# Token projections of two mixers, joined in pairs of 512 moving weight columns

## The reference

```
# first block, each of its two layers
h = rmsnorm(x, mix_pre_g)
proj = h @ w_in                  # 3860 columns, split among four heads groups:
#   gated delta net, differential attention (with rotary q, k),
#   state-space scan, mLSTM
# second block, each of its two layers
proj = modulate(x) @ w_in_2      # 3072 columns:
rq, rk, rv, rg, dq, dk, dv, sq, sk, sv = split(proj)
y = concat(retention(rotate(rq), rotate(rk), rv, rg),
           dilated_attention(rotate(dq), rotate(dk), dv),
           stick_breaking(sq, sk, sv)) @ w_out_2
```

## Time and profile before

| | |
|---|---|
| runs | 2170.27, 2171.44, 2171.54 us; median 2171.44 |
| span of the profiled execution | 2169.3 us; the page gives no whole time for it, the median lies 2.1 us above the span |
| PE busy | 2125.2 us (98%), 12850 matmuls |
| DVE busy | 1653.5 us (76%) |
| ACT busy | 1182.4 us (55%) |
| POOL busy | 73.5 us (3%) |
| HBM read | 444.42 MB, 205 GB/s over the span |

### The profile page before, as it was taken

One profiled execution on the slowest core, in us unless ns is written; L12 is line 12 of the kernel. 1 busy time (PEld: TensorE's weight loads), 2 busy tenths in 40 slices (PEclk: granted clock), 3 DMA queues, 4 the chain that ended last, 5 costly groups with the idle time before them and its releaser, 6 DMA issues.

```text
span 2169.3 us, 34586 instructions
## 1 busy us (share of the span) xinstructions
PE 2125.2 (98%) x12850; PEld 1864.8 (86%) x12850; DVE 1653.5 (76%) x2161; ACT 1182.4 (55%) x1589; POOL 73.5 (3%) x70
## 2 busy tenths in 40 slices
PE   8999999999999999999999999999999999999997
PEld 7888999888888889988888888988888888898886
DVE  6877897787778788977877877867787557876657
ACT  5545545654655574465556546546546445656544
POOL 0000200000000003000000000100000000000000
PEclk9999999999999999999999999999999999999999
DMA  8775322577487642238765775437764555443553
GB/s 313 292 281 204 128 79 98 214 282 279 169 325 267 260 156 98 79 112 315 267 255 215 285 280 205 137 105 281 277 252 171 194 200 213 156 136 137 183 194 145
DMA packets 59413, 446.65 MB, mean 206 GB/s; under 512 B 6977, under 2 KB 7361, under 8 KB 8897
## 3 DMA queue, kind: packets, MB, share of 16 engines
q1 hardware_dynamic: 59328, 445.50, 55.2%
HBM read 444.42 MB, written 1.05 MB: 205 GB/s over the span
## 4 chain that ended last, share of the span: by engine, by line
PE 88%; DVE 7%; ACT 3%; DMA 1%; issue 1%; POOL 0%; SPq 0%; DVEq 0%; ACTq 0%
PE ps L249 28%; PE ps L358 15%; PE ps L254 15%; PE ps L364 8%; PE ps L265 3%; PE ps L307 2%; PE ps L313 2%; PE ps L308 2%; PE ps L339 2%; PE ps L230 1%; PE ps L236 1%; PE ps L231 1%; DVE w_lo L206 1%; DMA raw<-in_g 1%; DVE tok L777 1%; PE ps L1196 1%
## 5 line engine op out<-in xcount | busy, mean ns | idle before, releaser
L206 DVE TENSOR_TENSOR w_lo<-raw,w_hi 128x1024 fp32r<-128x1024 f32 x670 | 813.4, 1235 | 274.6 <-ACT w_hi L199 273.8
L199 ACT ACTIVATE w_hi<-raw 128x1024 fp32r<-128x1024 f32 x670 | 693.7, 1052 | 411.2 <-PE ps L364 133.7
L249 PE MATMUL ps<-hT,w_hi 128*128 128x512 f32 x2688 | 671.3, 392 | 0.5 <-ACT w_hi L199 0.5
L249 PEld LDWEIGHTS ps<-hT,w_hi 128*128 128x128 f32 x2688 | 487.9, 189 | 91.4 <-ACT w_hi L199 1.1
L254 PEld LDWEIGHTS ps<-hT,w_lo 128*128 128x128 f32 x2688 | 366.7, 190 | 26.2
L254 PE MATMUL ps<-hT,w_lo 128*128 128x256 f32 x2688 | 374.8, 282 | 0.0
L358 PE MATMUL ps<-w_hi,act_hi 128*128 128x512 f32 x672 | 208.9, 392 | 0.0
L358 PE MATMUL ps<-w_hi,act_lo 128*128 128x512 f32 x672 | 207.6, 390 | 0.0
L364 PE MATMUL ps<-w_lo,act_hi 128*128 128x512 f32 x672 | 179.6, 389 | 0.0
L2081 DVE SCALAR_TENSOR_TENSOR arena<-arena,cond 128x1024 f32<-128x1024 f32 x144 | 168.5, 1221 | 2.7 <-DMA arena<-in_w_ada 2.7
L358 PEld LDWEIGHTS ps<-w_hi,act_lo 128*128 128x128 f32 x672 | 126.2, 188 | 27.5
(11 more groups left out here) (370 smaller groups left out, 2447.5 us busy)
## 6 DMA issues: line engine op xcount, KB each, us to landing
raw<-in_u SPq DMA_DIRECT2D x88, 1024.0 KB, 4.9
raw<-in_d SPq DMA_DIRECT2D x88, 1024.0 KB, 6.9
raw<-in_g SPq DMA_DIRECT2D x87, 1024.0 KB, 4.8
arena<-in_w_ada SPq DMA_DIRECT2D x48, 1536.0 KB, 7.5
raw<-in_w_in SPq DMA_DIRECT2D x54, 1024.0 KB, 4.9
raw<-in_w_out SPq DMA_DIRECT2D x16, 1024.0 KB, 4.9
rows<-in_rows SPq DMA_DIRECT2D x12, 1024.0 KB, 9.0
arena<-in_con SPq DMA_DIRECT2D x1, 1344.0 KB, 10.8
```

The source lines that it names most:

```text
L199: nc.scalar.activation(w_hi[:, buf, 0:width], raw[:, slot, half * UNIT:half * UNIT + width], ACT.Copy).then_inc(unit_hi, 1)
L206: nc.vector.tensor_tensor(w_lo[:, buf, 0:width], raw[:, slot, half * UNIT:half * UNIT + width], w_hi[:, buf, 0:width].bitcast(F32), ALU.su ...
L249: nc.tensor.matmul(o, h_[:, k, c], hT[:, :, 4 * half + k, :], start=(half == k == 0), stop=False)
```

## The change

In mixer 1 the token tiles 4 and 5 become a pair, in mixer 2 the pairs (2, 3), (4, 5), (8, 9) and (10, 11). The host joins the columns of two weight tiles and cuts the result by rows into four quarters, each of two 128-row chunks by 512 columns, of the same size as a unit; the DMAs and conversions stay as they are. `pair_unit` multiplies a quarter: for token tile 0 four hi matmuls of 512 columns and two lo, then the same for tile 1, 12 in all. Each token tile has a bank of its own. Tile 1's bank is the one that tile n - 1 used, so in the first quarter there is a wait for its copy (`freed`) ahead of token tile 1. At the end of token tile 0 in the last quarter `pair_first` is raised; `evict(n)` waits for it and copies 512 columns of token tile 0, `evict(n + 1)` waits for the end of the unit and copies token tile 1. In ScalarE's stream `evict(n)` of a pair moves behind the conversions of the last quarters and of the first unit or units after them.

```diff
+PAIRS1 = (4,)
+PAIRS2 = (2, 4, 8, 10)
...
+    def pair_unit(pe, B, j, banks, quarter, freed=None):
+        buf = home(B, j)
+        h_, l_ = (w[:, buf, :].rearrange("p (k n) -> p k n", k=2) for w in (w_hi, w_lo))
+        unit_ready(pe, unit_hi, B, j)
+        for tile in range(TILES):
+            o, c = ps[:, banks[tile], :], slice(tile * P, (tile + 1) * P)
+            if tile and freed:
+                freed()
+            for k in range(2):
+                nc.tensor.matmul(o, hT_hi[:, 2 * quarter + k, c], h_[:, k, :], start=(quarter == k == 0), stop=False)
+                nc.tensor.matmul(o, hT_lo[:, 2 * quarter + k, c], h_[:, k, :], start=False, stop=False)
+            if tile == 0:
+                unit_ready(pe, unit_lo, B, j)
+            for k in range(2):
+                last = nc.tensor.matmul(o, hT_hi[:, 2 * quarter + k, c], l_[:, k, :], start=False,
+                                        stop=(quarter == 3 and k == 1))
+            if tile == 0 and quarter == 3:
+                last.then_inc(pair_first, 1)
+        last.then_inc(unit_done, 1)
...
+                elif n in PAIRS1:
+                    pair_unit(pe, B, j, (6 + n % 2, 7 - n % 2), half, None if half else lambda: evicted(n - 1))
+                elif n - 1 in PAIRS1:
+                    pair_unit(pe, B, j, (7 - n % 2, 6 + n % 2), 2 + half)
...
+            elif n in PAIRS1:
+                a.wait_ge(pair_first, l * len(PAIRS1) + (PAIRS1.index(n) + 1))
...
-        evict(4)
         after(T1, "sums")
         nc.scalar.activation(gc, ps[:, 5, 0:24].rearrange("p (a b) -> p a b", a=2), ACT.Copy).then_inc(A1.done("gc"), 1)
         after(V1, "rs")
         nc.scalar.activation(rn, rn, ACT.Sqrt).then_inc(A1.done("root"), 1)
         hi(6)
+        evict(4)
         after(V1, "dec_g")
...
-        evict(2)
         hi(4, (0,))
         after(A2, "e_b")
         nc.scalar.activation(b3, b3, ACT.Ln, bias=one[:, 0:1]).then_inc(A2.done("l_b"), 1)
         hi(4, (1,))
+        evict(2)
         evict(3)
         hi(5)
+        hi(6)
         evict(4)
-        hi(6)
         evict(5)
...
+        hi(10)
         evict(8)
-        hi(10)
         evict(9)
...
+        hi(12)
         evict(10)
-        hi(12)
         evict(11)
```

More of the change, by code:

```diff
@@ L157, in build @@
     proj_evac = sem("proj_evac")
+    pair_first = sem("pair_first")
     pre_t = steps("pre_t", "trans0a trans0b trans1a trans1b")
@@ L1459, in mixer1_act @@
                          8: u[:, 6:8, PAD:], 10: u[:, 8:10, PAD:], 11: u[:, 10:12, PAD:]}
-        token_homes = {4: rope_in[:, :, 0:SEQ], 5: rope_in[:, :, SEQ:512], 12: v_d, 13: z_s, 14: o_m, 15: gate_g}
+        token_homes = {12: v_d, 13: z_s, 14: o_m, 15: gate_g}
         def evict(n):
@@ L1468, in evict @@
             bank = 6 + n % 2
-            if n == SMALL_AT:
+            if n in (4, 5):
+                last = nc.scalar.activation(rope_in[:, n - 4, :], ps[:, bank, :], ACT.Copy)
+            elif n == SMALL_AT:
                 last = nc.scalar.activation(small, ps[:, bank, 0:2 * SMALL].rearrange("p (a b) -> p a b", a=2), ACT.Copy)
@@ L2153, in project @@
                         entry_feature(pe, B, g, 4)
+                elif n in PAIRS2:
+                    pair_unit(pe, B, j, (4 + n % 2, 5 - n % 2), half_, None if half_ else lambda: evicted(n - 1))
+                elif n - 1 in PAIRS2:
+                    pair_unit(pe, B, j, (5 - n % 2, 4 + n % 2), 2 + half_)
                 else:
@@ L2300, in evict @@
         def evict(n):
-            a.wait_ge(unit_done, B + (ENDS2[n] + CREDIT))
-            two = ps[:, 4 + n % 2, :].rearrange("p (a b) -> p a b", a=2)
+            if n in PAIRS2:
+                a.wait_ge(pair_first, DEPTH * len(PAIRS1) + (l * len(PAIRS2) + (PAIRS2.index(n) + 1)))
+            else:
+                a.wait_ge(unit_done, B + (ENDS2[n] + CREDIT))
+            bank, tile = ps[:, 4 + n % 2, :], n % 2
+            two = bank.rearrange("p (a b) -> p a b", a=2)
             func, scale = ACT.Copy, 1.0
             if n < 2:
-                to, scale = sqk[:, 2 * n:2 * n + 2, :], 1.0 if n else 64.0 ** -0.5
+                to, from_, scale = sqk[:, 2 * n:2 * n + 2, :], two, 1.0 if n else 64.0 ** -0.5
             elif n < 6:
-                at = (n - 2 + 2) % 4 * SEQ
-                to = rot_in[:, :, at:at + SEQ]
+                at = n // 2 % 2 * 512
+                to, from_ = rot_in[:, tile, at:at + 512], bank
             elif n < 8:
-                to = v_b if n == 6 else v_2
+                to, from_ = v_b if n == 6 else v_2, two
             elif n < 10:
-                to = v_r[:, :, (n - 8) * SEQ:(n - 7) * SEQ]
+                to, from_ = v_r[:, tile, :], bank
             else:
-                to, func = g_r[:, :, (n - 10) * SEQ:(n - 9) * SEQ], ACT.Silu
-            nc.scalar.activation(to, two, func, scale=scale).then_inc(proj_evac, 1)
+                to, from_, func = g_r[:, tile, :], bank, ACT.Silu
+            nc.scalar.activation(to, from_, func, scale=scale).then_inc(proj_evac, 1)
         def hi(n, halves=(0, 1)):
@@ L2802, in column_tiles, with joined @@
                                 .reshape(L_, n // width, P, -1))
+def joined(tiles, first):
+    L_, n, p, _ = tiles.shape
+    for i in first:
+        both = np.concatenate([tiles[:, j].reshape(L_, p, KT, FB) for j in (i, i + 1)], 3)
+        tiles[:, i], tiles[:, i + 1] = (both[:, :, k:k + KT // 2].reshape(L_, p, -1) for k in (0, KT // 2))
+    return tiles
 def row_tiles(w):
@@ L2819, in layout @@
     big = [0, 256, 512, 1032, 1288, 2828, 3084, 2056, 3340, 2312, 2568, 1544, 1800, 3596, 768]
-    a["w_in"] = column_tiles(np.concatenate([w[:, :, c:c + 256] for c in big], 2))
+    a["w_in"] = joined(column_tiles(np.concatenate([w[:, :, c:c + 256] for c in big], 2)), [n - 1 for n in PAIRS1])
     ws = np.concatenate([w[:, :, 1024:1028], w[:, :, 3852:3856], w[:, :, 1028:1032], w[:, :, 2824:2828],
@@ L2825, in layout @@
     w = i["w_in_2"]
-    a["w_in_2"] = column_tiles(np.concatenate([w[:, :, c:c + 256] for c in
-                                               (2304, 2560, 1536, 1792, 0, 256, 2816, 2048, 512, 768, 1024, 1280)], 2))
+    a["w_in_2"] = joined(column_tiles(np.concatenate([w[:, :, c:c + 256] for c in
+                                                      (2304, 2560, 1536, 1792, 0, 256, 2816, 2048, 512, 768, 1024, 1280)],
+                                                     2)), PAIRS2)
     a["w_out_2"] = row_tiles(i["w_out_2"])
```

## The result

The changed kernel takes 2179.52 us in the median (2178.45 to 2180.84, 5 runs) against 2171.44 before: a ratio of 1.0039 with a 95% interval of 1.0028 to 1.005. It is slower, by more than the 0.2% that can be told, and above my range (2171.5 to 2177.8). The profiled execution took 2180.84 us, with a span of 2179.1: 9.8 us more than before, where the sum said 3.7. It is the slowest of the five; the median rose by 8.1. Three single executions further down took two to four times as long (4276 us with mixer 1 undone, 4729 with copy 10 early, 8110 with the pairs 8 and 10 alone); nothing here explains them, and medians and ranges are those of the other executions.

What follows compares the result with a forecast made beforehand. TensorE, 88% of the chain, was taken to bound the kernel. Mixer 1's +3.1 and mixer 2's +0.6 gave +3.7 us on a 2169.3 span, 2173.0; with 2.1 to the median, 2175.1 us (8 in 10: 2171.5 to 2177.8).

Steps and rivals of the forecast that it cites:

- Saved on TensorE: 12 matmuls of 512 columns for 24 of 256 save 0.15 us a changed unit, 6.0 us over 40 units.
- a saving of 2.5 ns a matmul: The skill's issue-gap rule on TensorE: 480 dropped matmuls save only 1.2 us, total about 2179 us; not followed.
- New wait 1: Mixer 1, middle of unit 4a: TensorE waits for tile 3's copy, stalls 2.16 us; +1.56 us a pass.
- rival 1: Mixer 1: GpSimd's later mask and rotations hold VectorE, 1.0 to 2.2 us a pass, 2177.1 to 2179.5 us; chance 0.20.
- New wait 2: Mixer 2, before tile 4: TensorE waits for tile 2's copy, stalls 2.49 us; net +1.10 us a pass.
- the pairs (8, 9) and (10, 11): Mixer 2: nine more units save 1.35 us a pass; entry waits covered; 0.57 us stall before the transposes after tile 11.
- the GpSimd wait: Mixer 2, after unit 5a: TensorE's old 0.34 us wait for GpSimd's mask goes, the mask being ready first.
- a drain behind each table load: ScalarE, end of mixer 2: skill's drain of about 1.38 us lengthens the stall 1.4 a pass, total near 2177.7; not followed.
- Rival 2: ScalarE's copies come in time, so the 6.0 us saving stands alone less 0.34: 2165.8 us; chance 0.06.
- Rival 3: Mixer 1 takes up its shift, leaving only +0.6 us: 2172.0 us; chance 0.13.
- Rival 4: The units are not joined in fact and the time stays at 2171.4 us; next to no chance.

Runs made afterwards that it cites:

- mixer 1 undone: Changed kernel with mixer 1's pair undone and its copies in their old places, mixer 2's pairs kept: 2173.25 us, ratio 1.0012 to the kernel before.
- copy 10 early: Changed kernel with mixer 2's copy of tile 10 put between unit 12's two conversions: 2178.62 us, ratio 1.0034 to the kernel before.
- pairs 8 and 10 alone: Kernel before with only mixer 2's pairs 8 and 10 joined, tile 10's copy between unit 12's two conversions: 2168.9 us, ratio 0.999.
- copies 2 and 3 early: Changed kernel with mixer 2's copies of tiles 2 and 3 moved ahead of unit 4b's conversion on ScalarE: 2175.17 us, ratio 1.0019 to the kernel before.
- fillers: Changed kernel with 8 extra 512-column matmuls for nothing at the head of unit 4a in both mixers: 2180.91 us, ratio 1.0046 to the kernel before.

## Why the prediction was wrong

**The step that failed** is "The granted clock reads 9 tenths or more, so the 2.4 GHz level, in all 40 slices, mixers with their short waits included; I charge nothing for it." The row was true and did not bear the conclusion. The longest wait of the mixers that it included is 1.3 us by the profile, or 1.48 from start to start less one pace, which is how I count stalls, and I was adding four of 2.2 to 2.5 us. Over all profiles, 26 passes had an idle TensorE of 2.06 to 2.50 us at these places, and 17 of them went on at 1.2 GHz for 3.4 us; 8 passes had one of 0.25 to 1.42 us there and none did. A stretch costs 1.55 to 1.6 us (3.60 against 2.03, 2.09 against 0.54), a little less than half of 3.4. Three of them make 4.7 of the 6.1 us that the sum was short. The forecast of 2175.1 with two or three of these added is 2178 to 2180.

**Saved on TensorE** held: the new matmuls start 0.227 us apart, and mixer 1 is 0.57 us ahead at the transposes where nothing waits, for 0.60. The Trainium skill (TensorE: Matmul & The Clock Gate, Wait — 56ns, not 53.3ns?) has N ÷ 1.2 GHz from start to start on the slow clock, 426.7 ns for 512 columns; the 0.42 to 0.43 us behind the stall agree. Its figure for the fast clock, 215.7 ns, does not: the rows have 227. The total that the prediction worked out from a saving of 2.5 ns a matmul (2175.1 + 4.8 is 2179.9, not 2179) lies at the measured time by luck, since 12.5 ns a matmul were saved all the same.

**New wait 1** held in place, cause and size (2.06 for 2.16). The pass then costs 2.03 at full clock (second pass with the copies 2 and 3 early, first with copy 10 early) where I had 1.56. Of the 0.47, 0.4 are the stretched VectorE operations. That is rival 1's place at a fraction of its price, and by another path: I feared the hold by the mask, and the mask came too late to hold anything. The Trainium skill (SBUF — State Buffer, SBUF: two separate sides) has the lock going to whichever starts first; here VectorE's small operation was over 0.48 us before the mask began, so these rows don't test it.

**New wait 2, the pairs (8, 9) and (10, 11)** held: 2.37 for 2.49, the GpSimd wait gone, 0.50 for 0.57 at the end, 0.47 to 0.54 a pass for 0.32 at full clock. No stall came ahead of tiles 6, 8 or 10. The longer total that the prediction gave for a drain behind each table load (2175.1 + 2 x 1.4 is 2177.9, not 2177.7) didn't come about either: 1.29 to 1.30 us go from a load's start to the activation's where that waits for nothing else.

**The rivals.** Rival 1's 2177.1 to 2179.5 reaches up to the measured 2179.52 for the wrong reason; the stretched VectorE operations account for 0.8 us, and that GpSimd stretches them is argued from the rows, not shown. Rival 2's premise, copies in time, I could make true by moving copies, and it yields 2.6 us (2.3 in the profile), not 6: of the 1.2 us saved in mixer 1, 0.9 go, most of it in VectorE's work, and of the 4.8 in mixer 2, 2.8 go, with a stall of 1.4 us kept in each pass. Rival 3 is out, mixer 1 passes its shift on in full. Rival 4 is out.

**The sum again**, with what was measured: 2 x 2.03 + 2 x 0.5 + 3 x 1.6 = 9.9 us, for 9.8 in the spans. The median rose by 1.7 less, about one stretch.

## What to carry to other kernels

When a change adds a stall of 2 us or more to a busy TensorE, price it with what may come behind it: the stall, and half of a 3.4 us stretch at 1.2 GHz in some of the executions. A page's row of 40 slices can't show that; look at the granted clock in stretches of 3 us behind each wait that is new. And before giving up a change for its waits, look at the order on the engine that is waited for: here moving four copies by an operation or two turned +8 us into -2.6.

## What the runs showed of the hardware

- The half-speed stretch is not certain. Behind a stall of 2.06 or 2.50 us mixer 1 fell in 10 of 12 passes, behind one of 2.37 us mixer 2's first pass in 6 of 7 and its second in 1 of 7. I found nothing in the rows before a stall that tells the passes apart; that stays open.
- It was 3.4 us long all 17 times. By the trace's record of the granted clock it starts from 0.25 us before the stall's end (the run with fillers, mixer 2) to 1.5 us behind it (the run with copies 2 and 3 early, mixer 1), so TensorE was mostly running again when the clock fell.
- In every profile with mixer 1's pair TensorE also idles ahead of the matmuls that L1271 has in the changed kernel, behind VectorE: 1.7 us a pass by the profile, and 1.86 to 1.90 from start to start less one pace (1.48 before). The clock stayed up in all 20 of these passes, though they come within 0.2 us of the 2.06 that fell in 8 passes of 10. Whether the length or the place makes the difference is not shown:

```profile
262.89 1.09 PE L1271 MATMUL ps<-base,arena 128*128 128x128 f32 x8 [1.70 <-DVE arena L1883]
```

- More work can be faster: mixer 1 with eight matmuls for nothing in its stall takes 1.6 us less a pass than with the stall empty and the clock falling, and as much as with the stall empty and the clock staying up (2.03).
